# The opening of a two-block transformer kernel: unread products of ones at its start, squares added on VectorE, the first weight panel in two halves

## What is computed

```
def rms_norm(x, g):
    xf = x.astype(jnp.float32)
    y = xf * lax.rsqrt(jnp.mean(xf * xf, axis=-1, keepdims=True) + RMS_EPS)
    return (y * g.astype(jnp.float32)).astype(x.dtype)

h = rms_norm(x, mix_norm_g[l])
proj = h @ w_in
```

## Time and profile before

| | us |
|---|---|
| median of three runs (lowest, highest) | 1003.07 (1001.24, 1003.3) |
| the profiled execution | 1002.95 |
| its span | 1001.1 |
| PE busy | 978.0 (98%) |
| VectorE busy | 695.7 (69%) |
| ACT busy | 537.4 (54%) |
| GpSimd busy | 35.5 (4%) |

### The profile page before, as it was taken

One profiled execution on the slowest core, in us unless ns is written; L12 is line 12 of the kernel. 1 busy time (PEld: TensorE's weight loads), 2 busy tenths in 40 slices (PEclk: granted clock), 3 DMA queues, 4 the chain that ended last, 5 costly groups with the idle time before them and its releaser, 6 DMA issues.

```text
span 1001.1 us, 20611 instructions
## 1 busy us (share of the span) xinstructions
PE 978.0 (98%) x8646; PEld 949.8 (95%) x8646; DVE 695.7 (69%) x855; ACT 537.4 (54%) x689; POOL 35.5 (4%) x28
## 2 busy tenths in 40 slices
PE   6998999999999999999999999999999999999998
PEld 5998898999999999999889999999999999999998
DVE  4668754656788988999887655556877867555553
ACT  5565645456665555467745544435666764444432
POOL 0025050000000000000000000000000000000000
PEclk9999999999999999999999999999999999999999
DMA  7643433333745565455343665555543135555551
GB/s 271 216 167 123 169 100 117 122 128 132 264 170 182 192 213 200 152 185 194 127 156 107 227 205 189 174 209 192 182 169 127 43 127 209 188 203 198 172 206 43
DMA packets 24833, 168.97 MB, mean 169 GB/s; under 512 B 2752, under 2 KB 3264, under 8 KB 4800
## 3 DMA queue, kind: packets, MB, share of 16 engines
q1 hardware_dynamic: 24192, 165.82, 47.4%
q10 hardware_dynamic: 576, 2.20, 0.6%
HBM read 166.96 MB, written 1.05 MB: 168 GB/s over the span
## 4 chain that ended last, share of the span: by engine, by line
PE 80%; DVE 12%; ACT 4%; issue 2%; DMA 1%; DVEq 0%; SPq 0%; ACTq 0%
PE G L594 14%; PE G L595 13%; PE G L596 13%; PE D L594 8%; PE D L595 8%; PE D L596 8%; DVE wlo L1799 4%; PE M L595 2%; PE M L594 2%; PE M L596 2%; ACT whi L1282 2%; PE M L812 1%; PE D L1141 1%; PE M L642 1%; DMA raw<-wall_dram 1%
## 5 line engine op out<-in xcount | busy, mean ns | idle before, releaser
L1799 DVE TENSOR_TENSOR wlo<-raw,whi 128x2048 fp32r<-128x2048 f32 x155 | 354.3, 2291 | 120.7 <-ACT whi L1282 120.5
L594 PE MATMUL G<-xh,whi 128*128 128x256 f32 x1280 | 362.1, 283 | 4.4 <-DVE xl L1820 2.9
L595 PE MATMUL G<-xl,whi 128*128 128x256 f32 x1280 | 355.6, 278 | 0.0
L596 PE MATMUL G<-xh,wlo 128*128 128x256 f32 x1280 | 355.5, 278 | 0.0
L1282 ACT ACTIVATE whi<-raw 128x2048 fp32r<-128x2048 f32 x155 | 295.5, 1909 | 58.6 <-PE D L596 47.4
L594 PEld LDWEIGHTS G<-xh,whi 128*128 128x128 f32 x1280 | 241.3, 189 | 12.6 <-DVE wlo L1799 7.4
L595 PEld LDWEIGHTS G<-xl,whi 128*128 128x128 f32 x1280 | 240.9, 188 | 1.1 <-issue 1.0
L596 PEld LDWEIGHTS G<-xh,wlo 128*128 128x128 f32 x1280 | 241.1, 188 | 0.0
L594 PE MATMUL D<-hh,whi 128*128 128x256 f32 x672 | 186.3, 277 | 0.8 <-issue 0.8
L596 PE MATMUL D<-hh,wlo 128*128 128x256 f32 x672 | 185.9, 277 | 0.0
L595 PE MATMUL D<-hl,whi 128*128 128x256 f32 x672 | 185.9, 277 | 0.0
(11 more groups left out here) (398 smaller groups left out, 1374.0 us busy)
## 6 DMA issues: line engine op xcount, KB each, us to landing
raw<-wall_dram SPq DMA_DIRECT2D x155, 1024.0 KB, 4.9
x<-x_dram SPq DMA_DIRECT2D x4, 256.0 KB, 5.0
mem<-mem_dram ACTq DMA_DIRECT2D x1, 1024.0 KB, 5.0
out_dram<-x SPq DMA_DIRECT2D x4, 256.0 KB, 2.2
poolw<-pool_w_dram ACTq DMA_DIRECT2D x1, 768.0 KB, 6.5
cst<-cst_dram SPq DMA_DIRECT2D x1, 448.0 KB, 11.9
lora<-lora_dram SPq DMA_DIRECT2D x1, 256.0 KB, 11.2
sgw<-sg_w_dram SPq DMA_DIRECT2D x1, 256.0 KB, 12.0
```

Source lines behind the costliest of these rows:

```text
L594: mm(out, w_h, hi, start=start, stop=False, skip_group_check=skip)
L595: mm(out, w_h, lo, start=False, stop=False, skip_group_check=skip)
L596: return mm(out, w_l, hi, start=False, stop=stop, skip_group_check=skip)
L1799: signal(tt(wlo[:, pan.slot, 0:w], raw[:, pan.slot, 0:w], f32(whi[:, pan.slot, 0:w]), SUB), "w_lo")
```

## The change

It touches the opening only, in six places.

- A piece of the tile `sig`, 128 x 512, is set to 1.0 by VectorE's first instruction, and serves as the ones of the opening. With that, TensorE's first wait is no longer for cst. It starts with three unread products of ones (`warm_start(3)`), and waits for cst only behind the six that follow the sums.
- VectorE adds quarters 1 and 2 of the squares to quarter 0, and TensorE makes four products (k-tiles 0 and 1 after the additions, 6 and 7 after the last square).
- x's quarter 1 is loaded by ACT's queue, ahead of cst and par.
- The first panel is loaded, and split by ACT and VectorE, in two halves, k-tiles 0 to 3 and 4 to 7 of both output tiles (`first_half`). The first half is split on both engines ahead of the root, the second half behind it.
- The order of scalings, subtractions and splits of the first norm is another on both engines; the first panel's products wait for `w_lo_first`, and from the third quarter on for `w_lo`.
- The late tables masks, sgb and lvl share one semaphore, ld_tables; who waited for one of them waits for all three.

The core of the diff:

```diff
+    def first_half(w, half):
+
+        return w[:, 0, :].rearrange("p (n k) -> p n k", n=2)[:, :, half * D // 2:(half + 1) * D // 2]
...
-        for i in range(4):
+        for i in (0, 2, 3):
             sp.dma_start(x[:, 2 * i:2 * i + 2, :], A["x"][:, 2 * i:2 * i + 2, :]).then_inc(S(f"x_moved{i}"), 16)
-        for p in range(SLOTS):
+        for half, landed in enumerate(("w_first", "w_land0")):
+            sp.dma_start(first_half(raw, half), A["wall"][0].rearrange("p (n k) -> p n k", n=2)
+                         [:, :, half * D // 2:(half + 1) * D // 2]).then_inc(S(landed), 16)
+        for p in range(1, SLOTS):
             load(Pan(p), A["wall"][p])
...
+                if count == XLN["rw"] and at == 2:
+                    pe.wait_ge(S("w_lo"), 1)
...
-        pe.wait_ge(S("ld_cst"), 16)
...
-        def warm_start():
-            for _ in range(6):
-                mm(flat(DB[0])[:, 0:384], ones, cst[:, CC["ident"]:CC["ident"] + 384], skip_group_check=True)
+        first_ones = sig[:, 0, 0:P]
+
+        def warm_start(products):
+            for _ in range(products):
+                mm(flat(DB[0])[:, 0:384], first_ones, sig[:, 0:2, :].rearrange("p a t -> p (a t)")[:, 0:384],
+                   skip_group_check=True)
...
             if n == 0:
-                for k in range(KT):
-                    pe.wait_ge(S("sq"), k // 2 + 1)
-                    ins = mm(M[1][:, 0, :], ones, wk[:, k, :], start=k == 0, stop=k == KT - 1)
+                for k in (0, 1, 6, 7):
+                    if k == 0:
+                        pe.wait_ge(S("sq_sum"), 1)
+                    if k == 6:
+                        pe.wait_ge(S("sq"), 4)
+                    ins = mm(M[1][:, 0, :], first_ones, wk[:, k, :], start=k == 0, stop=k == 7)
...
             if n == 0:
-                warm_start()
+                warm_start(6)
+                pe.wait_ge(S("ld_cst"), 16)
...
+        pe.wait_ge(S("zeros"), 1)
+        warm_start(3)
         walk(pe, {"begin": begin, ...
...
         tables("natural_log_exp_and_others")
+        act.dma_start(x[:, 2:4, :], A["x"][:, 2:4, :]).then_inc(S("x_moved1"), 16)
...
-                if i == 0:
+                if i == 1:
                     split_to(2)

         def norm(n):
             squares(n)
+            act.wait_ge(S("w_first"), 16)
+            signal(fn(first_half(whi, 0), first_half(raw, 0), ACT.Copy), "w_hi_first")
             root(n)
-            if n == 0:
-                split_to(1)
+            act.wait_ge(S("w_land0"), 16)
+            signal(fn(first_half(whi, 1), first_half(raw, 1), ACT.Copy), "w_hi")
+            done[0] = 1
             high(n)
...
         def norm(n):
+            for i in (1, 2):
+                add_squares(wk, "sq", 0, i, 2, "sq_sum")
+            dve.wait_ge(S("w_hi_first"), 1)
+            signal(tt(first_half(wlo, 0), first_half(raw, 0), f32(first_half(whi, 0)), SUB), "w_lo_first")
             root(n)
             a, b, _, (gain, g0) = NORMS[n]
             for i in range(4):
                 scaled(wk, x, rstd, gain, i, "nrm", g0)
-                if i == 0:
-                    split_to(1)
-                for q in ((0,), (), (1,), (2, 3))[i]:
+                for q in ((), (0, 1), (), (2, 3))[i]:
                     low(b + q + 1, q, wk[:, 2 * q:2 * q + 2, :], xh, xl)
+                if i == 1:
+                    dve.wait_ge(S("w_hi"), 1)
+                    signal(tt(first_half(wlo, 1), first_half(raw, 1), f32(first_half(whi, 1)), SUB), "w_lo")
+                    done[0] = 1
...
+        signal(nc.vector.memset(sig[:, 0:2, :], 1.0), "zeros")
         signal(nc.vector.memset(z_rw[:, :, 0:1], 0.0), "zeros")
         nc.vector.memset(cum[:, :, 0:1], 0.0)
         dve.wait_ge(S("ld_par"), 16)
```

More of the change, by code:

```diff
@@ L434, in build @@
     FNORM = [1, 4, 6]
-    SUMS = (1, 2, 3, 4, 5, 6)
+    SUMS = (0, 1, 2, 3, 4, 5, 6)
     IN_B = ("wo", "mkv0", "mkv1", "kv")
@@ L509, in run @@
                 load(Pan(p), A["wall"][p - skip])
-        for i in range(4):
+        for i in (0, 2, 3):
             sp.dma_start(x[:, 2 * i:2 * i + 2, :], A["x"][:, 2 * i:2 * i + 2, :]).then_inc(S(f"x_moved{i}"), 16)
-        for p in range(SLOTS):
+        for half, landed in enumerate(("w_first", "w_land0")):
+            sp.dma_start(first_half(raw, half), A["wall"][0].rearrange("p (n k) -> p n k", n=2)
+                         [:, :, half * D // 2:(half + 1) * D // 2]).then_inc(S(landed), 16)
+        for p in range(1, SLOTS):
             load(Pan(p), A["wall"][p])
         for name, dst, src in (("lora_pool", lora[:], A["lora"]),
-                               ("masks", cst[:, CC["suffix"]:NCC], A["cst"][:, CC["suffix"]:NCC]),
-                               ("sgw_mem", sgw[:], A["sg_w"]), ("sgb", sgb[:], A["sg_b"]), ("lvl", lvl[:], A["lvl"])):
+                               ("tables", cst[:, CC["suffix"]:NCC], A["cst"][:, CC["suffix"]:NCC]),
+                               ("sgw_mem", sgw[:], A["sg_w"]), ("tables", sgb[:], A["sg_b"]), ("tables", lvl[:], A["lvl"])):
             sp.dma_start(dst, src).then_inc(S("ld_" + name), 16)
@@ L534, in inv_mask @@
             if g == 0:
-                pool.wait_ge(S("ld_lvl"), 16)
+                pool.wait_ge(S("ld_tables"), 48)
                 pool.wait_ge(S("rw_prod"), 8)
@@ L567, in rw_scale @@
             pool.wait_ge(S("ld_sgw_mem"), 16)
-            pool.wait_ge(S("ld_masks"), 16)
+            pool.wait_ge(S("ld_tables"), 48)
             tt(sgw[:], sgw[:], c("incl").unsqueeze(1).broadcast_to([P, 4, P]), ALU.mult).then_inc(S("sg_tril"), 1)
@@ L639, in norm_stat @@
             if n == 0:
-                for k in range(KT):
-                    pe.wait_ge(S("sq"), k // 2 + 1)
-                    ins = mm(M[1][:, 0, :], ones, wk[:, k, :], start=k == 0, stop=k == KT - 1)
+                for k in (0, 1, 6, 7):
[4 more added lines that the diff above has]
+                    ins = mm(M[1][:, 0, :], first_ones, wk[:, k, :], start=k == 0, stop=k == 7)
             elif n == 1:
-                pe.wait_ge(S("sq_sum"), 1)
+                pe.wait_ge(S("sq_sum"), 2)
                 pe.wait_ge(S("sq"), 8)
@@ L683, in panel @@
                 return
-            pe.wait_ge(S("w_lo"), p + 1)
+            if p == 0:
+                pe.wait_ge(S("w_lo_first"), 1)
+            else:
+                pe.wait_ge(S("w_lo"), p + 1)
             if name in PAIRS:
@@ L982, in sb_q @@
         def sb_q(h):
-            pe.wait_ge(S("ld_masks"), 16)
+            pe.wait_ge(S("ld_tables"), 48)
             pe.wait_ge(S("sb_sp"), h + 1)
@@ L1407, in panel @@
                 if i == 0:
-                    act.wait_ge(S("zeros"), 1)
+                    act.wait_ge(S("zeros"), 2)
                 dst = z_rw[:, 2 * i:2 * i + 2, 1:T + 1]
@@ L2160, in sg_mix @@
             dve.wait_ge(S("sg_mixed"), 1)
-            dve.wait_ge(S("ld_sgb"), 16)
+            dve.wait_ge(S("ld_tables"), 48)
             for n in range(2):
```

## The result

The changed kernel is slower: 1004.16 us in the median of 11 runs (1002.29 to 1005.48) against 1001.31 us (1000.5 to 1003.3, 11 runs) for the kernel before, a ratio of 1.0024 with a 95% interval of 1.0016 to 1.0031. The time lies in the stated range, but the forecast was + 0.14 us, no measurable change. The profiled execution took 1004.19 us, its span is 1002.4 us.

A forecast was written before the change was run, and what follows sets the result against it. TensorE was taken as bound from 25 us on, leaving only the second panel's start to change: root 12.92 + 11.87 = 24.79 us against 24.65, so 1002.95 + 0.14 = 1003.1 us; whole range 1000.9 to 1004.5 us.

The forecast's parts named there:

- The clock at the sums: TensorE's sums of squares: half clock after a pause of about 4 us, 3.62 us long, root at 12.92 us.
- That the opening products might not lift the level: TensorE's start: three products last 3.8 us, while the level had taken 5.3 us of work to rise.
- That the pause of 2.42 us at 15.8 us was short enough to do no harm: TensorE before the first panel, kernel before: full clock right behind this pause, so it cost nothing.
- par and the additions: VectorE before the sums: par in at 7.3 us, two additions of 0.687 us done at 9.13, sums from 9.27 us.
- the rival with par: Opening: par later than 7.3 us delays sums and root equally; at 8.5 us 1004.3 us in all; chance 0.13.
- The halves: First panel: half splits hidden before the root at either clock; second panel 11.87 us behind the root instead of 12.73.
- The unread products: Six on TensorE behind the sums: over at 17.5 us, before the first panel's first product at 17.67 us.
- The wait for cst: TensorE behind the unread products: cst landed long before, so no delay.
- the shared semaphore of the tables: Late tables: lvl is issued last anyway and first used far later than 30 us, so cost 0.
- The sum at the second panel: Start of the second weight panel's products: 24.79 us against 24.65, + 0.14 us.
- The rest of the program follows at the same distance: Behind the second panel's start, near 25 us: everything shifts by the same amount as that start.
- The base: The profiled execution of the kernel before, 1002.95 us, taken 0.12 under a median of 1003.07; + 0.14 added to it.

The follow-up runs named there:

- x on SP's queue: The changed kernel with all four parts of x on SP's queue again, cst and par alone on ScalarE's: 1002.49 us, ratio 1.0002 to the kernel before.
- opening products alone: The kernel before with only a memset of sig and three opening products of it ahead of the wait for cst: 1001.43 us, ratio 0.9991.
- eight products again: The changed kernel with eight products of ones, each pair waiting for its own square, and no additions on VectorE: 1001.1 us, ratio 0.9990.
- halves alone: The changed kernel with eight products of ones, x on SP's queue and no opening products: 1001.7 us, ratio 0.9994 to the kernel before.
- Additions alone: The kernel before with only the additions of squares on VectorE and four products of ones: 1004.17 us, ratio 1.0020.

## Why the prediction was right and wrong

*The clock at the sums: right.* The prediction said that the pause would bring the sums to 1.2 GHz and put the opening's price there. Granted was 0.50 throughout the sums of the changed kernel. All five profiles with additions behind a pause of 3 us or more, or behind no work at all, had their eight records in 3.61 to 3.78 us; the one whose pause was filled had them in 1.99 us.

*That the opening products might not lift the level: wrong in the change's profile* (0.86 in the pause means that it had been up), with no effect on the sum, as it fell in time; right in that of x on SP's queue, where no fall is recorded. *That the pause of 2.42 us at 15.8 us was short enough to do no harm: luck of that execution.* In the second profile of the kernel before and in that of the opening products alone, 2.41 us in the same place cost the clock.

*par and the additions: right in kind, mis-sized by 0.5 us.* The sums were to start at 9.27 us and started at 9.77 us. par's first user ran at 8.01 us instead of 7.32 us; the additions took 1.41 us, as forecast (0.687 us each). As the last of ScalarE's three transfers par was 1.8 us later than before, not 1.1. With 0.16 us more for the sums themselves (3.78 for 3.62) 0.67 us of lateness stands in the root: 13.59 for 12.92 us. This is the mechanism of the rival with par, in a size between forecast and rival.

*The halves: right at half clock.* 11.76 us from root to second panel for 11.87; half splits of 1.06 and 1.22 us, both hidden behind the slow sums. That they are hidden in either case was wrong: with the early root of eight products again, ScalarE's half split held it by 0.77 us. The unread products ended at 18.36 us, not at 17.5, just as the first xl was there. The wait for cst cost nothing, as the first product of the panel follows them without a pause; the shared semaphore of the tables was not tested by itself.

*The sum at the second panel* was + 0.14 and came to + 0.70 us.

*The rest of the program follows at the same distance: failed by 0.6 us* in the profiles. I had left out that VectorE and GpSimd hold each other up from 71 us on, and that their starts lie a tenth or two of a us apart. The split at 83 us took 3.37 us instead of 2.48, and TensorE waited 1.05 us for it instead of 0.18. This worse order stands in seven of the ten profiles that leave GpSimd's order alone, also in those with an earlier root; only the two of the kernel before and that of the halves alone have the better one.

*The base: failed, and it is the largest part.* The sum was set against an execution of 1002.95 us, 1.64 us above the median of 1001.31 us that eleven executions gave, and took for the kernel before what that one had: the level up only at 10.9 us in the sums. That the time lies in the stated range is luck to that extent: the same range, laid around the lower median, would have ended at 1002.9 us. In four profiles with eight products and no opening ones the root was at 11.92, 11.85, 11.50 and 11.03 us, and the medians of the kernel before were 1001.31 us beside the change and 1001.86, 1002.09 and 1002.87 us beside the later runs. Additions alone, which in the profile put the root only 0.63 us behind that of the first profile, cost 2.0 us by the ratio. Of the measured 2.4 us (0.24% by the ratio; the medians lie 2.85 us apart) the two profiles of the change and before account for 1.3 us. The rest goes with the clock of whole executions: the granted clock was 0.997 or less in 8 of the 11 executions of the change (1003.96 to 1005.48 us; the three others, at 0.998, took 1002.29, 1002.31 and 1003.62 us) and in 19 of the 94 of the kernel before beside the later runs. Which stretches these are was not seen in more than one profile of the change.

*The chances.* With 0.80 on no measurable change and 0.08 on slower I was too sure. The forecast named the right mechanism for a loss of 1.0 us at the root and set a gain of 0.86 us against it. The gain came (0.97 us in the profiles); the loss was larger (1.67 us), and both were reckoned from one execution.

## What to carry to other kernels

Fewer products are no gain if they must wait for another engine: what counts is when the last one can start and at which clock it runs. Work that is to lift the clock must reach to the work that shall use it; in front of a pause of 4.3 us it was worth nothing that could be measured, without the pause it was worth about 0.9 us (0.9991). A split hidden behind a slow stretch stands on the path once that stretch is fast. A sum against one profile is no better than that execution: ask of each gain or loss under a few us which of the profile's half-clock stretches the next execution will have.

## What the runs showed of the hardware

The same pause of TensorE, 2.42 and 2.41 us in two executions of one kernel, left the clock up in the first and brought it to 0.50 in the second; with opening products alone, 2.41 us in that place brought it to 0.50 too. VectorE and GpSimd with two-operand work on 128 partitions hold each other up: 2.29 and 3.26 us for one and the same split, 1.28 and 3.39 us for one and the same product, by who starts first. The Trainium skill, page "TensorE: Matmul & The Clock Gate", Part 1, has it that the moment of the rise varies from run to run; here sixteen records from about 5.5 us on took 6.33, 6.40 and 5.42 us in three executions, so it does.
